# Feed-forwards with context by seven block products: two stages of a fused fp32 network on TensorE

## The chip, the cores and the metric

The kernel runs on one core of a Trainium2 chip. The metric is the device time of one execution in microseconds (us); lower is better. It is one launch, all weights come from HBM, and each fp32 operand of TensorE is split in a high part (of type fp32r) and a low part (the rest).

## What is computed

Two residual blocks in a row on 512 image tokens with 256 context tokens, model width 1024, hidden width 2816 (22 feature tiles of 128). A block has token mixers and gated feed-forwards, with modulation vectors made from a condition. Four feed-forwards are in the program. Two of them are applied to image and context tokens together (768 tokens): the first of block one, and that of the first layer of block two. These are the two that are changed.

```python
def rms_norm(x):
    xf = x.astype(jnp.float32)
    return (xf * lax.rsqrt(jnp.mean(xf * xf, axis=-1, keepdims=True) + RMS_EPS)).astype(x.dtype)

def modulate(x, shift, scale):
    return x * (1.0 + scale) + shift

def swiglu(x, wg, wu, wd):
    return (jax.nn.silu(x @ wg) * (x @ wu)) @ wd

def half_ffn(h, shift, scale, gate, wg, wu, wd):
    return h + 0.5 * gate * swiglu(modulate(rms_norm(h), shift, scale), wg, wu, wd)
```

## The kernel before

The stages run in the order filters, block1_ffn1, block1_mix, block1_ffn2, block2_mix0, block2_ffn0, block2_mix1, block2_ffn1, final. Each engine has a program of its own, and semaphores order them; the order of the work is written by hand. A matrix product is done as three products: high weights with high data, high weights with low data, low weights with high data.

Weights come as tiles of 128 x 1024 fp32 (512 KB) through one stream in HBM, in the order in which they are used. SyncE loads a tile in one of two raw buffers, ScalarE copies its high part in a ring of four (split_tile, L513), VectorE subtracts to get the low part (dve_low_tile, L527), and only then the raw buffer is free for the next load. In some stages GpSimd makes the low parts instead (L2780). Beside it SyncE loads the tiles of the modulation weights in two further buffers; VectorE multiplies each with the condition and sums it up, once for each of one or two vectors (dve_mod_tile, L570).

A feed-forward with context (pe_ffn, L826; act_ffn, L843; dve_ffn, L882) works in thirds of 8, 8 and 6 feature tiles. For each feature there is a gate tile and an up tile. A tile has 8 steps over the model width, three products in each, and two matmuls of 384 columns in each product, since 768 tokens lie in two banks of PSUM: 48 matmuls a tile. ScalarE takes silu of the gate (L852), VectorE multiplies it with the up part out of PSUM (L900), ScalarE and VectorE split the result in the hidden buffers (L859, L907). After a third come the 8 down tiles, each over the features of the third, and VectorE adds each output to the stream H (dve_residual, L952). PSUM has two slots of two banks for this, used in turn. Two modulation tiles go with each feature, and one with each output, in those loops for which the plan has them.

The stage begins with the norm: TensorE sums squares over the partitions, ScalarE makes the reciprocal root (L648, L651), VectorE scales a tile (L793, L798), ScalarE adds the shift and writes the high part (L732, L738), VectorE the low part (L776, L780). TensorE takes the first gate and up tile together, step by step, as the eight tiles of the input come (pe_pair, L435, matmuls at L457); all other tiles go through pe_tile (L410, matmuls at L427). The first four weight tiles are loaded and split during the filters stage (L1538, low parts on GpSimd at L2771), between the two layers of a small network whose sines ScalarE computes (L1544).

## Time and profile before

| | |
|---|---|
| time, median of 3 runs | 3512.42 us (3509.75 to 3512.66) |
| span of the profiled execution | 3513.3 us |
| TensorE busy | 3314.9 us (94%), 18356 matmuls |
| VectorE busy | 1987.9 us (57%) |
| ScalarE busy | 1152.1 us (33%) |
| GpSimd busy | 131.8 us (4%), 64 instructions |
| loads | 392 weight tiles and 168 modulation tiles of 512 KB |

The profile is of one execution. Its page names engines PE (TensorE's matmuls), PEld (its weight loads, which overlap the matmuls), DVE (VectorE), ACT (ScalarE), POOL (GpSimd) and SP (SyncE; SPq is its queue of DMA issues). Matmuls are pipelined and their ends are modelled, so that the duration of one in a row is longer than the pace at which they follow each other; the pace is the length of a stretch over the number in it. Stages are found by time: the first feed-forward with context runs from 160.5 to 712.8 us, the second from 2191 to 2743.7 us.

### The profile page before, as it was taken

The page shows a single profiled execution, that of the slowest core. Times are in us where ns is not written, and L with a number is a line of the kernel's source. Part 1 is how long each engine was busy: PE and PEld are TensorE (multiplying, and loading weights), DVE is VectorE, ACT ScalarE, POOL GpSimd, SP SyncE. Part 2 cuts the span into 40 slices and gives each one's busy share as a digit, 9 for nine tenths or more (in the row PEclk, how much of TensorE's full clock was granted, in tenths as well). Part 3 has the DMA queues.
Part 4 walks back from the last instruction along what each step waited for, and adds up shares of the span by engine and source line. Part 5 has one row for each costly group of instructions (what it writes and reads, how often), then busy time and mean ns, then how long its engine had stood idle before and what let it go on. Part 6 is the DMA issues. An engine that isn't in the chain of part 4 may idle for free.

```text
span 3513.3 us, 49004 instructions
## 1 busy us (share of the span) xinstructions
PE 3314.9 (94%) x18356; PEld 2879.2 (82%) x18356; DVE 1987.9 (57%) x2943; ACT 1152.1 (33%) x1604; POOL 131.8 (4%) x64
## 2 busy tenths in 40 slices
PE   6899999999999999999899889999999999789998
PEld 3599999988888887888688657999999767578887
DVE  6556443457766658884569573653433467653334
ACT  2221211235541133223435272311212344543223
POOL 3000000000000000000011100000000111000000
PEclk8799999999999999999989899999999989999999
DMA  5233332331122235553221202333322211113232
GB/s 217 100 120 133 125 130 78 115 108 38 36 82 81 82 127 178 191 192 108 68 72 31 77 3 72 105 134 120 132 96 66 81 43 43 43 60 98 93 96 96
DMA packets 101989, 339.95 MB, mean 97 GB/s; under 512 B 10351, under 2 KB 21487, under 8 KB 100432
## 3 DMA queue, kind: packets, MB, share of 16 engines
q1 hardware_dynamic: 82888, 301.91, 25.9%
q10 hardware_dynamic: 18952, 36.01, 2.9%
q8 instruction: 99, 1.62, 0.2%
q14 instruction: 50, 0.41, 0.0%
HBM read 323.73 MB, written 14.16 MB: 96 GB/s over the span
## 4 chain that ended last, share of the span: by engine, by line
PE 79%; DVE 10%; ACT 5%; issue 3%; DMA 2%; ACTq 1%; POOL 0%; SPq 0%; DVEq 0%; POOLq 0%
PE ps L427 62%; PE ps L473 5%; PE ps L457 2%; PE ps L1094 1%; ACT pr L2563 1%; DMA hyena_k<-fst 1%; PE ps L1956 1%; PE ps L1943 1%; PE ps L1042 1%; DVE u_ex L1240 1%; DVE u_Z L1354 1%; ACT pT L2570 1%; ACT wr_hi L524 1%; PE ps L1515 1%; DMA raw<-in_stream 1%
## 5 line engine op out<-in xcount | busy, mean ns | idle before, releaser
L524 ACT ACTIVATE wr_hi<-raw 128x1024 fp32r<-128x1024 f32 x388 | 411.8, 1061 | 601.1 <-PE ps L427 547.2
L534 DVE TENSOR_TENSOR wr_lo<-raw,wr_hi 128x1024 fp32r<-128x1024 f32 x348 | 426.2, 1225 | 80.6 <-ACT wr_hi L524 48.9
L900 DVE TENSOR_TENSOR ff_raw<-ps,ff_gate 128x768 f32<-128x768 f32 (+1 forms) x88 | 72.6, 825 | 571.0 <-PE ps L427 568.1
L427 PE MATMUL ps<-xx_hi,wr_hi 128*128 128x512 f32 x992 | 393.1, 396 | 2.0 <-ACT ff_gate L852 1.9
L427 PE MATMUL ps<-xx_lo,wr_hi 128*128 128x512 f32 x992 | 388.8, 392 | 0.0
L427 PE MATMUL ps<-xx_hi,wr_lo 128*128 128x512 f32 x992 | 388.5, 392 | 0.0
L427 PE MATMUL ps<-xa_hi,wr_hi 128*128 128x384 f32 x1344 | 341.0, 334 | 0.1
L427 PE MATMUL ps<-xa_lo,wr_hi 128*128 128x384 f32 x1344 | 341.0, 334 | 0.0
L427 PE MATMUL ps<-xa_hi,wr_lo 128*128 128x384 f32 x1344 | 341.0, 334 | 0.0
L578 DVE CUSTOM_DVE_ANT_0 ps<-raw,cb 128x1024 f32<-128x1024 f32 x240 | 295.4, 1231 | 54.1 <-DMA raw<-in_mod_stream 39.3
L427 PE MATMUL ps<-hid_hi,wr_hi 128*128 128x384 f32 (+1 forms) x1056 | 316.2, 353 | 3.8 <-DVE H L961 2.0
L427 PE MATMUL ps<-hid_lo,wr_hi 128*128 128x384 f32 (+1 forms) x1056 | 315.6, 352 | 0.0
L427 PE MATMUL ps<-hid_hi,wr_lo 128*128 128x384 f32 (+1 forms) x1056 | 315.5, 352 | 0.0
L427 PEld LDWEIGHTS ps<-xa_hi,wr_hi 128*128 128x128 f32 x1344 | 242.4, 188 | 0.6 <-issue 0.6
L427 PEld LDWEIGHTS ps<-xa_hi,wr_lo 128*128 128x128 f32 x1344 | 242.6, 188 | 0.0
L427 PEld LDWEIGHTS ps<-xa_lo,wr_hi 128*128 128x128 f32 x1344 | 242.6, 188 | 0.0
L859 ACT ACTIVATE hid_hi<-ff_raw 128x768 f32 (+1 forms) x88 | 65.2, 741 | 507.4 <-DVE ff_raw L900 507.3
L427 PEld LDWEIGHTS ps<-xx_hi,wr_hi 128*128 128x128 f32 x992 | 187.5, 189 | 44.3 <-issue 5.1
L427 PEld LDWEIGHTS ps<-xx_hi,wr_lo 128*128 128x128 f32 x992 | 187.3, 189 | 40.1
L427 PEld LDWEIGHTS ps<-xx_lo,wr_hi 128*128 128x128 f32 x992 | 187.5, 189 | 39.8 <-issue 0.8
L427 PEld LDWEIGHTS ps<-hid_hi,wr_hi 128*128 128x128 f32 x1056 | 193.0, 188 | 19.9 <-DVE hid_lo L907 2.7
L427 PEld LDWEIGHTS ps<-hid_hi,wr_lo 128*128 128x128 f32 x1056 | 193.2, 188 | 13.7
(417 smaller groups left out, 5327.3 us busy)
## 6 DMA issues: line engine op xcount, KB each, us to landing
raw<-in_stream SPq DMA_DIRECT2D x392, 512.0 KB, 3.6
raw<-in_mod_stream SPq DMA_DIRECT2D x168, 512.0 KB, 4.5
...
```

The costliest lines, as they stand in the source:

```text
L427: last = pe.matmul(gslot(slot)[:, col:col + n], w, rhs[part], start=(bi == 0 and pi == 0), stop=(bi == len(blocks) - 1 and pi == 2))
L457: last = pe.matmul(gslot(slots[t])[:, col:col + n], w, rhs[part], start=(k == 0 and pi == 0), stop=(k == steps - 1 and pi == 2))
L473: last = pe.matmul(gslot(slot)[:, col:col + n], w, rhs[part], start=(k == 0 and pi == 0), stop=(k == KC - 1 and pi == 2))
L524: act.activation(wr_hi[:, s, :], raw[:, s % RAW, :], ACT.Copy).then_inc(tile_hi, 1)
L534: dve.tensor_tensor(wr_lo[:, s, :], raw[:, s % RAW, :], wr_hi[:, s, :], ALU.subtract).then_inc(tile_lo, 1)
L578: ins = dve.tensor_tensor_reduce(out=product, in0=raw[:, RAW + place, :], in1=cb[:, v, :], scale=1.0, scalar=0.0, op0=ALU.mult, op1=ALU.ad ...
L859: act.activation(hid[0][:, bass.ds(i * 2 + q, 1), 0:n], ff_raw[:, q:q + 1, 0:n], ACT.Copy).then_inc(hhi_ready, 1)
L900: dve.tensor_tensor(parts(ff_raw[:, q, :], with_ctx), gparts(slot, with_ctx), parts(ff_gate[:, q, :], with_ctx), ALU.mult).then_inc(slot_f ...
L1042: last = pe.matmul(m[:, j * NX + c * HD:j * NX + (c + 1) * HD], Z[r, c * CH:(c + 1) * CH], queries[r, c * per:(c + 1) * per, 0 if bw else ...
L1094: last = pe.matmul(m[:, j * NX + c * HD:j * NX + (c + 1) * HD], Z[r, c * CH:(c + 1) * CH], queries[r, c * per:(c + 1) * per, 0 if bw else ...
L1240: dve.tensor_tensor(x, cum, a, ALU.subtract).then_inc(ex_in, 1)
L1354: dve.tensor_tensor(z[:, :, h, :], x[:, :, h, :], side[:, :, h, :], ALU.mult).then_inc(z_ready, 1)
```

## The change

In the two feed-forwards with context the products for a gate and an up tile are no longer done tile by tile. The pair of weight tiles is seen as a 2 x 2 matrix of blocks (gate or up; first or second half of the model width), the input as 2 x 2 blocks (half of the model width; half of the tokens), and the product of the two is made with seven block products and sums of blocks in place of eight. In detail:

- The input is prepared once in seven versions (units) of 4 x 384: some are blocks of it, four are made by 16 subtractions of 384 on GpSimd (pool_pair_norm). ScalarE and VectorE split all 28 parts in high and low. xn holds the scaled and shifted input, xs the seven versions.
- The weights of a pair are prepared in every round: the pair is loaded in both raw buffers, GpSimd makes four block sums of 512 (pool_pair_sums), ScalarE and VectorE split seven units of 512 in place of two tiles of 1024 (act_weights, dve_weights). Each unit of the next pair is written in its place of the ring once the product of this round that used it is done.
- A round on TensorE (pe_pair_round) is seven products of 4 steps x 3 matmuls of 384 columns. ScalarE copies the first three results out of PSUM, further products are added by TensorE in the same banks, and VectorE adds three banks to the copies (prod_summed); then silu, the two multiplications and the split of the hidden tile in two halves.
- Features go in groups of 4, 2, 4, 4, 4, 4 in place of 8, 8, 6, each group followed by its down products: four stream tiles, each for two outputs, over the features of the group. The sums into H come 48 times a stage in place of 24.
- Two modulation tiles stay with each feature, with two vectors or one; after the very first round they come behind the round's work, in all others ahead of it. Further ones lie in the down parts of some groups.
- Weights of gate and up come from an array of their own (pairs), the rest from the stream; TensorE's loops of these stages are written out. The first pair is prepared in the filters stage, with its low parts on GpSimd, and the pair for the second of these stages at the end of block2_mix0.

The diff, cut to its core:

```diff
+        def act_weights(act, tally, r, i):
+
+            sums = {1: 1, 2: 3, 4: 2, 5: 4}
+            if i in sums:
+                act.wait_ge(sum_ready, 4 * r + sums[i])
+            elif i == 0 or i == 6:
+                act.wait_ge(landed[i // 6], pair_landed(r, tally.n.get("tile_hi", 0)))
+            act.activation(unit_at(wr_hi, i), unit_raw(i), ACT.Copy).then_inc(unit_hi, 1)
+            act.wait_ge(unit_hi, PAIR_UNITS * r + i + 1)
+
+        def dve_weights(dve, r, i):
+            dve.wait_ge(unit_hi, PAIR_UNITS * r + i + 1)
+            dve.tensor_tensor(unit_at(wr_lo, i), unit_raw(i), unit_at(wr_hi, i), ALU.subtract).then_inc(unit_lo, 1)
+
+        def pool_pair_sums(pool, r, tiles):
+
+            gate_a, gate_b, up_a, up_b = raw[:, 0, 0:512], raw[:, 0, 512:1024], raw[:, 1, 0:512], raw[:, 1, 512:1024]
+            if r:
+                pool.wait_ge(unit_lo, PAIR_UNITS * (r - 1) + 2)
+            for s in range(RAW):
+                pool.wait_ge(landed[s], pair_landed(r, tiles))
+            nc.gpsimd.tensor_tensor(s_sum[:, :], up_a, up_b, ALU.add).then_inc(sum_ready, 1)
+            pool.wait_ge(sum_ready, 4 * r + 1)
+            nc.gpsimd.tensor_tensor(up_a, gate_a, up_a, ALU.subtract).then_inc(sum_ready, 1)
+            pool.wait_ge(sum_ready, 4 * r + 2)
...
+            pool.wait_ge(unit_lo, PAIR_UNITS * r + 1)
+            nc.gpsimd.tensor_tensor(gate_a, s_sum[:, :], gate_a, ALU.subtract).then_inc(sum_ready, 1)
...
+            pool.wait_ge(unit_lo, PAIR_UNITS * r + 4)
+            nc.gpsimd.tensor_tensor(gate_b, gate_b, gate_a, ALU.subtract).then_inc(sum_ready, 1)
...
+        def dve_pair_norm(dve, tally, which, shift, scale, gain=None, before=None):
...
+            for m in range(KC):
+                scaled(m)
+                if m:
+                    low((m - 1) // 4, (m - 1) % 4)
+            low(1, 3)
+            for u in range(2, PAIR_UNITS):
+                for j in range(4):
+                    low(u, j)
...
+        def pe_pair_round(pe, tally, r, which, first, begin):
+
+            for i in range(PAIR_UNITS):
+                pe.wait_ge(unit_lo, PAIR_UNITS * r + i + 1)
...
+                elif i == 1 and r:
+                    pe.wait_ge(prod_summed, 3 * r)
+                elif i == 2:
+                    pe.wait_ge(prod_copied, 3 * r + 1)
+                elif i == 3 and r:
+                    pe.wait_ge(prod_summed, 3 * (r - 1) + 1)
+                elif i == 4:
+                    pe.wait_ge(prod_copied, 3 * r + 3)
+                elif i == 5:
+                    pe.wait_ge(prod_copied, 3 * r + 2)
+                elif i == 6:
+                    pe.wait_ge(prod_summed, 3 * r + 2)
+                w_hi, w_lo = unit_at(wr_hi, i), unit_at(wr_lo, i)
+                for j in range(4):
+                    if first:
+                        pe.wait_ge(xs_ready, 4 * PAIR_UNITS * which + 4 * i + j + 1)
+                    for pi, (w, part) in enumerate(((w_hi, 0), (w_hi, 1), (w_lo, 0))):
+                        last = pe.matmul(pair_bank(r, i), w[:, j * P:(j + 1) * P], xs[part][:, i, j, :],
+                                         start=(i in (0, 1, 3) and j == 0 and pi == 0), stop=(j == 3 and pi == 2),
+                                         skip_group_check=True)
+                last.then_inc(prod_done, 1)
...
+            if not copied:
+                for n in range(3):
+                    act_prod_copy(act, tally, r, n)
+            high(0)
+            high(1)
+            act_gate(0)
+            high(2)
+            high(3)
+            if not then_down:
+                high(4)
+            act_gate(1)
+            if then_down:
+                high(4)
+            high(5)
+            act_hid(1)
+            act_hid(0)
+            high(6)
...
+        def dve_pair_round(dve, tally, r, f, then_down, later):
...
+            summed(0, gate0)
+            low(0)
+            low(1)
+            summed(1, up1)
+            low(2)
+            low(3)
+            summed(2, gate1)
+            low(4)
+            dve.wait_ge(prod_summed, 3 * r + 2)
+            dve.wait_ge(silu_ready, 2 * r + 2)
+            dve.tensor_tensor(gate1, up1, gate1, ALU.mult).then_inc(gated_half, 1)
+            low(5)
+            low_half(1, half_lo)
+            dve.wait_ge(prod_done, PAIR_UNITS * (r + 1))
+            dve.tensor_tensor(gate0, pair_bank(r, 6), gate0, ALU.mult).then_inc(gated_half, 1)
+            low_half(0, hid_ready)
+            tally.passed("hid_ready")
+            low(6)
+            if later is not None:
+                later()
...
+            def load_pair(r):
+                for s in range(RAW):
+                    sp.wait_ge(unit_lo, PAIR_UNITS * r + s - 1)
+                    sp.dma_start(raw[:, s, :], ins["pairs"][2 * r + s]).then_inc(landed[s], 16)
...
+PAIR_GROUPS = (4, 2, 4, 4, 4, 4)
+PAIR_UNITS = 7
+PAIR_MODS = (((2, 0), (2, 0), (2, 2), (1, 1), (1, 1), (1, 0)), ((2, 2), (2, 0), (1, 0), (1, 0), (1, 0), (1, 0)))
```

## Rows read from the trace of the kernel before

**Rows 1.** The page, busy us (share of the span) xinstructions of each engine.

```profile
PE 3314.9 (94%) x18356; PEld 2879.2 (82%) x18356; DVE 1987.9 (57%) x2943; ACT 1152.1 (33%) x1604; POOL 131.8 (4%) x64
```

**Rows 2.** The chain that ended last: start us, us, what.

```profile
160.58 19.47 PE ps L457 x96
180.04 532.72 PE ps L427 x3072
...
2210.88 532.73 PE ps L427 x3072
```

**Rows 3.** Windows, the first feed-forward with context: length, busy us of each engine, clock.

```profile
160.50:712.80 552.30, 552.22 (x3169) 551.78 (x3170) 275.23 (x368) 128.68 (x137) 0.00 (x0) 0.99 0.34 115
```

**Rows 4.** Timeline, start of the second such stage: start us, us, engine, line.

```profile
2188.93 0.75 DVE L793 SCALAR_TENSOR_TENSOR xt<-H,scv,rstd 128x512 f32<-128x512 f32 x1 [2.92 <-ACT rstd L651]
...
2191.18 0.98 PE L457 MATMUL ps<-xa_hi,wr_hi 128*128 128x384 f32 x2 [4.23 <-ACT xa_hi L738]
...
2197.10 0.51 PE L457 MATMUL ps<-xa_hi,wr_hi 128*128 128x384 f32 x2
```

**Rows 5.** Groups by line and form, first stage: xcount, busy us, mean ns, idle before.

```profile
L578 DVE CUSTOM_DVE_ANT_0 ps<-raw,cb 128x1024 f32<-128x1024 f32 x80 | 98.4, 1230 | 20.1 <-DMA raw<-in_mod_stream 16.6 <-DVE mods L590 2.4 <-DVE xa_lo L780 0.3
```

**Rows 6.** Durations of 512 and 384 wide work: two groups by form, two timeline rows.

```profile
L2135 DVE TENSOR_TENSOR y_lo<-hyp,y_hi 128x512 fp32r<-128x512 f32 x8 | 5.5, 684 | 0.0
...
L859 ACT ACTIVATE hid_hi<-ff_raw 128x512 f32 x44 | 27.9, 634 | 190.7 <-DVE ff_raw L900 190.6
...
1798.20 0.56 DVE L1354 TENSOR_TENSOR u_Z<-u_ex,gk 128x384 f32<-128x384 f32 x1
1798.68 0.55 DVE L1354 TENSOR_TENSOR u_Z<-u_ex,gq 128x384 f32<-128x384 f32 x1
```

**Rows 7.** Timeline of VectorE, a modulation tile with two vectors and what follows.

```profile
249.09 1.23 DVE L578 CUSTOM_DVE_ANT_0 ps<-raw,cb 128x1024 f32<-128x1024 f32 x1
...
250.41 1.23 DVE L578 CUSTOM_DVE_ANT_0 ps<-raw,cb 128x1024 f32<-128x1024 f32 x1
...
251.94 0.96 DVE L907 TENSOR_TENSOR hid_lo<-ff_raw,hid_hi 128x768 f32 x1 [0.25 <-DVE modacc L578]
```

**Rows 8.** Groups by form, GpSimd.

```profile
L2780 POOL TENSOR_TENSOR wr_lo<-raw,wr_hi 128x1024 fp32r<-128x1024 f32 x40 | 96.5, 2414 | 2821.7 <-ACT wr_hi L524 2821.7
L1600 POOL TENSOR_TENSOR ssq_first<-ssq_first,sq_first 128x768 f32<-128x768 f32 x7 | 13.7, 1961 | 25.3 <-ACT sq_first L1583 25.3
```

**Rows 9.** Timelines of GpSimd and VectorE, three places where both work.

```profile
47.40 6.28 POOL L1597 TENSOR_TENSOR H<-H,pos_col 128x512 f32<-128x512 f32 x4
48.02 1.64 DVE L1642 TENSOR_TENSOR fe<-fa 128x512 f32<-128x512 f32 x1
...
60.53 1.94 POOL L1600 TENSOR_TENSOR ssq_first<-ssq_first,sq_first 128x768 f32<-128x768 f32 x1 [6.85 <-ACT sq_first L1583]
60.84 2.71 DVE L578 CUSTOM_DVE_ANT_0 mod_out<-raw,cb 128x1024 f32<-128x1024 f32 x1
...
1791.93 2.42 POOL L2780 TENSOR_TENSOR wr_lo<-raw,wr_hi 128x1024 fp32r<-128x1024 f32 x1 [6.14 <-ACT wr_hi L524]
1792.56 0.96 DVE L2344 SCALAR_TENSOR_TENSOR oacc<-ps,oacc 128x768 f32<-128x768 f32 x1 [0.41 <-PE ps L2167]
```

**Rows 10.** A load on SyncE's queue, and the issues: KB each, median us to landing.

```profile
2185.88 0.33 SPq L2747 DMA_DIRECT2D raw<-in_stream  x1
...
raw<-in_stream SPq DMA_DIRECT2D x392, 512.0 KB, 3.6
```

**Rows 11.** Timeline of the filters stage, VectorE and ScalarE around the second layer's sine.

```profile
22.48 0.43 DVE L1625 TENSOR_SCALAR fh<-fh 128x512 f32<-128x512 f32 x1
...
24.52 1.06 ACT L1538 ACTIVATE wr_hi<-raw 128x1024 fp32r<-128x1024 f32 x1 [7.48 <-DMA raw<-in_stream]
...
26.90 1.91 ACT L563 ACTIVATE cb<-cb 128x2048 f32<-128x2048 f32 x1
...
28.84 0.63 ACT L1544 ACTIVATE fh<-fh 128x512 f32<-128x512 f32 x1
```

481 lines of the change are left out of this document (398 added, 83 removed).

## Prediction, written before the changed kernel was run

> **What bounds the kernel now.** I read the page's busy table first: TensorE is busy 94% of the span, VectorE 57%, GpSimd 4% [rows 1]. The chain of work that ended last says where that is a bound: in each of the two feed-forwards with context the chain is one unbroken piece of 3072 matmuls in 532.7 us, after a piece of 96 in 19.5 us that starts it [rows 2]. So there TensorE issues one 384-column matmul every 532.72/3072 = 173.4 ns and waits for nobody. The window of the first stage shows the rest: in 552.3 us VectorE works 275 us, ScalarE 129 us, GpSimd not at all [rows 3]. VectorE is half idle, but it is the only other engine with much work, and in the first feed-forward the modulation products alone (80 of 1.23 us) are a third of it [rows 5]. What is to be asked of the change is not whether TensorE gets less work (it does), but whether VectorE, GpSimd and the loads still keep up with it.
>
> **Removed.** A pair of gate and up tiles takes 2 x 8 x 2 x 3 = 96 matmuls; seven products of 4 steps x 3 take 84. Down products stay 24 features x columns as before (22 x 8 x 2 x 3 = 1056). Over 22 pairs and two stages 528 matmuls go: 528 x 0.1734 = 91.6 us. The pace should hold, since it does not depend on the loop around it (the same 173.4 ns in both stages). A round of 84 now lasts 14.57 us, and all of the following has to fit beside that.
>
> **VectorE in a round.** Durations: 512-wide subtraction 0.69 us, 384-wide 0.55, and such instructions follow each other 0.08 us closer than their durations [rows 6]. Seven weight units 7 x 0.61 = 4.3; three sums from PSUM, two multiplications, two low halves, 7 x 0.47 = 3.3; two modulation tiles of two vectors 2 x 2.85 = 5.7 (with one vector 3.1, a product less for each tile, 1.32), read from start to next start [rows 7]; a wait of about 0.65 for ScalarE's high half in the last half tile. Sum 14.0 us (11.4 with one vector) of 14.57. Alone it would fit, just.
>
> **GpSimd in a round.** Four 512-wide operations. Its 1024-wide took 2.41 us and 768-wide 1.96 [rows 8], so 1.15 to 1.25 each, 4.8 us a round. First what the trace shows of the two engines together: with GpSimd running from 60.53 to 62.47, a modulation product of VectorE that starts at 60.84 takes 2.71 us in place of 1.23, so it lost 1.48 of the 1.63 us of overlap; a subtraction in SBUF took 1.64 us beside a stream of GpSimd work, in place of 0.69; an operation with one operand in PSUM took 0.96 beside GpSimd, its usual time [rows 9]. So lows, low halves, one multiplication and modulations (11.5 us a round) take turns with GpSimd, the sums from PSUM don't. About 1 us of the 4.8 falls beside those; I add 3.5. The Trainium skill (SBUF — State Buffer, "SBUF: two separate sides") says the shared port pair is an exclusive lock for a whole instruction against VectorE operations with two SBUF inputs; by it all 4.8 would be added, 1.2 us more for each of the some ten rounds bound by VectorE, 12 us in all: 3551. The row has the loss slightly under that, and the sum goes by the row.
>
> **The loop through the load.** The pair for the round after next is loaded once the last unit of this one is split. From there: issue and landing (0.33 and 3.6 [rows 10], 4.1 with the way to both queues), two sums on GpSimd, the third (which waits for VectorE's unit 0), ScalarE's unit 2 (0.63), VectorE's units 2 and 3, the fourth sum, ScalarE's and VectorE's unit 5, then the low half, the last multiplication, ScalarE's half tile, the low half, unit 6. Counted on one clock from "unit 6 split": loads landed 4.1; sums 5.3 and 6.5 to 7.5; third sum 8.6 (9.9 with two vectors); unit 2 at 9.9 (11.1); unit 3 10.5 (11.7); fourth sum 11.7 (12.9); unit 5 13.3 (14.5); unit 6 16.1 (17.2). So a round is 16.1 us with one vector and 17.2 with two, against TensorE's 14.57.
>
> **What of that reaches TensorE.** Product 6 waits for the second PSUM sum (8.0 or 9.2 on that clock; allowed 12.5 us into TensorE's round), and product 2 waits for ScalarE's copy of product 0, which is queued behind the previous round's unit 6 (16.6, or 17.7; allowed 4.2 into the next round). After a group of down products VectorE starts 2.1 us behind. A group of four with one vector: behind 4.1, 5.7, 5.7 us at its next rounds; stalls 0, 0, 1.5, 1.5: 3 us. With two vectors: 4.7, 5.9, 5.9; stalls 1.45, 2.65, 1.75, and 2.5 at the down products' last feature (hidden features come ready 22 us after the round began, the first three features cover 3.1): 8.3, taken as 9 since the group before it leaves VectorE later. The group of two has only one feature (1.04 us) as cover: 5.1, and 1.4 more because its outputs come every 2.08 us against 1.9 of VectorE's work: 6.5. First stage: 6.5 + 9 + 3 x 3 = 24.5. Second: 6.5 + 4 x 3 = 18.5.
>
> **The start of a stage.** Before, the first matmul comes 2.25 us after VectorE's first instruction, and 96 take 19.4 us, 2.7 over their pace, a part of them at the 1.2 GHz level (0.98 us for two, later 0.51) [rows 4]. After, VectorE makes 8 scaled tiles and 28 low parts, ScalarE 16 biased and 28 high parts, GpSimd 16 sums of 384 (0.93 each). For the first eight steps VectorE needs 1.18 + 0.47 and gives way to one GpSimd operation (0.85 less gaps): 2.25 us each, to 19.7 us. Then 20 low parts and 10 to 11 GpSimd operations in turn: to 38.9. Only behind them in its queue stand the first sums: product 6 starts at 41.2 and ends at 43.2. Without the turn-taking it would be 35. The 84 matmuls need 2.25 + 14.57 = 16.8; loss 26.4, less the 2.7 of before: 23.7. Then VectorE has two rounds of modulations in a row (11.4 plus two GpSimd sums): the next product 6 waits to 65.2 where it could start at 55.7: 9.5. The third round 2.65, the last 1.75 + 2.5. A stage's first group: 40.1 us, two of them 80.2. Bounds: 26 without turn-taking, 46 if VectorE loses every turn.
>
> **The filters.** The second pair of raw tiles falls away there: ScalarE waited 7.5 us for it, and the second layer's sine at 28.84 was queued behind it and the 1.9 us silu, while its argument was ready at 22.9 [rows 11]. Gain 6, less 2 for three more weight copies and GpSimd's chain in front of the absolute values: 4 us (bounds 7 and -2). Down instructions: 24 more residuals per stage, 1.2 us each, lie beside 4.16 us of matmuls per output: nothing, as long as VectorE is not already behind.
>
> **Sum.** 3513.3 - 91.6 + 80.2 + 24.5 + 18.5 - 4 = 3540.9 for the profiled execution, which lies 0.9 over the median: 3540.
>
> **Rivals.**
> A, faster: turn-taking costs little, since GpSimd's sums fall into VectorE's waits for TensorE. Then only the start costs, 26 to 27 us per stage, and 1 at each group of two: 3513 - 92 + 55 - 4 = 3472; with half of the turn-taking 3500. For it: VectorE's own sum, 14.0 of 14.57. Against it: rows 9, and the 16 us loop for the load, which is there with few turns too (15.1).
> B, slower still: TensorE's clock. It ran at its 2.4 GHz level throughout the two stages and at 1.2 for 5.6 us after each gap in front of them [rows 3, 4]. With gaps of 2 to 9 us in some twelve rounds, 5.6 us at half rate cost 2.8 each; most lie inside rounds that wait for VectorE anyway. It decides from gaps in front of down products (five of them) and at the start: 15 to 35 more, 3565.
> C, none to see: the bounds of the start (26) with the groups as worked out: 3513 - 92 + 52 + 43 - 4 = 3512.
> D, the seven products don't keep the pace of 173.4 ns, each having its own start and one bank: 2% on 3700 matmuls would be 13 us. Nothing in the rows speaks for it.
>
> **Numbers.** Forecast 0.44 (3515 to 3560), A 0.34 (3468 to 3505), B with D 0.14, C 0.08. A change of 0.2%, 7 us, is about what a measurement can tell. Slower 0.56 (nearly all of the forecast, B and D), same 0.09 (most of C), faster 0.35 (A and a rest of C). The range takes in A and B: 3465 to 3578. The forecast's own range is 3515 to 3560.
>
> **What would show it.** In the profile after: 528 matmuls fewer at the same 173 ns; TensorE waiting for VectorE's sums (product 6) and ScalarE's copies (product 2), in the first group of each stage for over 25 us; GpSimd at about 370 us busy in place of 132 (176 pair sums of 1.2 and 32 of 0.93 on top); VectorE's 512-wide subtractions at a mean well over 0.69 us in these stages (0.9 or more), its PSUM sums at 0.55. Wrong if the subtractions keep 0.69, if rounds come every 14.6 us in groups two to six, or if the first round ends under 36 us after VectorE's first instruction; then it is A.

## The result, and the profile after

The changed kernel takes 3595.69 us (median of four, 3589.35 to 3601.39), the kernel before on the same chip 3511.09 (3508.38 to 3512.66): ratio 1.0248, 95% interval 1.0225 to 1.0270. It is slower by some 85 us. The profiled execution has a span of 3589.2 us, 75.9 over that of before.

Page of the changed kernel: span, busy us (share) xinstructions of each engine, to be held against [rows 1].

```profile
span 3589.2 us, 48360 instructions
...
PE 3277.0 (91%) x17828; PEld 2814.0 (78%) x17828; DVE 2307.1 (64%) x3500; ACT 1362.6 (38%) x2097; POOL 430.1 (12%) x275
```

The 528 matmuls are gone. Window of the first feed-forward with context (length, then busy us of PE, PEld, DVE, ACT, POOL, granted clock), to be held against [rows 3]:

```profile
154.60:760.50 605.90, 545.84 (x2912) 527.50 (x2912) 438.56 (x653) 235.59 (x384) 145.49 (x100) 0.94 0.33 108
```

VectorE went from 275 to 439 us in that stage, GpSimd from 0 to 145, the granted clock from 0.99 to 0.94, and TensorE, which waited for nobody, now waits. TensorE's longest waits (us in total, times, longest):

```profile
PE ps L1135 <- ACT gh L1168: 45.4, 31, 2.5
PE ps L1135 <- DVE xs_lo L1070: 29.5, 24, 7.4
PE ps L440 <- DVE hs_lo L1307: 28.9, 12, 4.8
...
PE ps L1135 <- DVE gh L1313: 13.8, 7, 5.7
```

L1135 is the products' line, L440 the down products'. The first wait is product 2 for ScalarE's copy of product 0, the second the start of a stage, the third the first output of each of twelve down groups, the last one shown product 6 for the PSUM sums.

From the starts of TensorE's rounds I take one number per piece of a stage, its *lateness*: time until the next piece starts, less its matmuls at 173.4 ns. A one-vector group is one whose modulation tiles are multiplied for one vector. Four rows of such a group, the starts of its second, third and fourth round and of its down products:

```profile
571.14 0.33 PE L1135 MATMUL ps<-xs_hi,wr_hi 128*128 128x384 f32 x1
...
586.79 0.34 PE L1135 MATMUL ps<-xs_hi,wr_hi 128*128 128x384 f32 x1
...
605.13 0.33 PE L1135 MATMUL ps<-xs_hi,wr_hi 128*128 128x384 f32 x1
...
620.79 0.33 PE L440 MATMUL ps<-hs_hi,wr_hi 128*128 128x384 f32 x1
```

The rounds took 15.65, 18.34 and 15.66 us against 14.57: late by 1.1, 3.8 and 1.1. Summed over both stages, with what the prediction's steps give in the same pieces:

| us, both stages | first round | second round | other 40 rounds | down products | sum |
|---|---|---|---|---|---|
| predicted | 52.8 | 19.0 | 36.3 | 20.5 | 128.6 |
| measured | 49.0 | 23.6 | 65.2 | 45.2 | 183.0 |

Of the 183.0, some 33 are matmuls that follow each other at 0.32 us in place of 0.173, TensorE's lower clock level: 11.7 in the first two columns, 12.4 in the other rounds, 8.8 in the down products. The account closes: 91.6 removed, 183.0 added, 5.3 of before's own lateness gone, 10.3 less outside the two stages: +75.8 against 75.9 measured.

### The profile page after: what moved, and what is told of

It reads as the page before. It is cut to its first block, busy times and chain, and to the rows that moved or that the text cites. A ratio compares the mean times of both kernels' runs of the same rounds, so it can differ in the third digit from the quotient of the medians.

```text
span 3589.2 us, 48360 instructions
## 1 busy us (share of the span) xinstructions
PE 3277.0 (91%) x17828; PEld 2814.0 (78%) x17828; DVE 2307.1 (64%) x3500; ACT 1362.6 (38%) x2097; POOL 430.1 (12%) x275
## 4 chain that ended last, share of the span: by engine, by line
PE 62%; DVE 18%; ACT 8%; issue 7%; DMA 3%; POOL 2%; ACTq 1%; SPq 0%; DVEq 0%; POOLq 0%
PE ps L440 40%; PE ps L1135 6%; PE ps L486 5%; DVE wr_lo L979 2%; ACT hs_hi L1185 1%; PE ps L1483 1%; ACT wr_hi L974 1%; DVE xs_lo L1070 1%; POOL raw L995 1%; ACT pr L2952 1%; DMA hyena_k<-fst 1%; DMA raw<-in_pairs 1%; PE ps L2345 1%; PE ps L2332 1%; PE ps L470 1%
## 5 line engine op out<-in xcount | busy, mean ns | idle before, releaser
L1135 PE MATMUL ps<-xs_hi,wr_hi 128*128 128x384 f32 x1232 | 436.4, 354 | 93.6 <-ACT gh L1168 45.4
L1135 PE MATMUL ps<-xs_hi,wr_lo 128*128 128x384 f32 x1232 | 427.4, 347 | 0.0
L1135 PE MATMUL ps<-xs_lo,wr_hi 128*128 128x384 f32 x1232 | 427.4, 347 | 0.0
L440 PE MATMUL ps<-xx_hi,wr_hi 128*128 128x512 f32 x992 | 393.4, 397 | 1.7 <-ACT ff_gate L857 1.7
L440 PE MATMUL ps<-xx_lo,wr_hi 128*128 128x512 f32 x992 | 389.5, 393 | 0.0
L440 PE MATMUL ps<-xx_hi,wr_lo 128*128 128x512 f32 x992 | 389.0, 392 | 0.0
L1135 PEld LDWEIGHTS ps<-xs_hi,wr_hi 128*128 128x128 f32 x1232 | 242.0, 196 | 122.4 <-issue 75.9
L587 DVE CUSTOM_DVE_ANT_0 ps<-raw,cb 128x1024 f32<-128x1024 f32 x240 | 305.3, 1272 | 19.2 <-DMA raw<-in_mod_stream 8.0
L543 DVE TENSOR_TENSOR wr_lo<-raw,wr_hi 128x1024 fp32r<-128x1024 f32 x216 | 264.4, 1225 | 64.5 <-ACT wr_hi L533 48.7
L979 DVE TENSOR_TENSOR wr_lo<-raw,wr_hi 128x512 fp32r<-128x512 f32 x258 | 213.0, 836 | 47.4 <-ACT wr_hi L974 42.6
L1135 PEld LDWEIGHTS ps<-xs_lo,wr_hi 128*128 128x128 f32 x1232 | 243.1, 197 | 0.0
L1135 PEld LDWEIGHTS ps<-xs_hi,wr_lo 128*128 128x128 f32 x1232 | 242.8, 197 | 0.0
L440 PEld LDWEIGHTS ps<-xx_hi,wr_hi 128*128 128x128 f32 x992 | 187.3, 189 | 43.9 <-issue 4.8
L440 PEld LDWEIGHTS ps<-xx_hi,wr_lo 128*128 128x128 f32 x992 | 187.3, 189 | 40.2
L440 PEld LDWEIGHTS ps<-xx_lo,wr_hi 128*128 128x128 f32 x992 | 187.5, 189 | 39.8 <-issue 0.8
L440 PE MATMUL ps<-hs_hi,wr_hi 128*128 128x384 f32 x704 | 184.2, 343 | 31.3 <-DVE hs_lo L1307 28.9
L440 PE MATMUL ps<-hs_lo,wr_hi 128*128 128x384 f32 x704 | 182.6, 341 | 0.0
L440 PE MATMUL ps<-hs_hi,wr_lo 128*128 128x384 f32 x704 | 182.4, 340 | 0.0
```

The costliest lines, as they stand in the source:

```text
L440: last = pe.matmul(gslot(slot)[:, col:col + n], w, rhs[part], start=(bi == 0 and pi == 0), stop=(bi == len(blocks) - 1 and pi == 2))
L543: dve.tensor_tensor(wr_lo[:, s, :], raw[:, s % RAW, :], wr_hi[:, s, :], ALU.subtract).then_inc(tile_lo, 1)
L587: ins = dve.tensor_tensor_reduce(out=product, in0=raw[:, RAW + place, :], in1=cb[:, v, :], scale=1.0, scalar=0.0, op0=ALU.mult, op1=ALU.ad ...
L979: dve.tensor_tensor(unit_at(wr_lo, i), unit_raw(i), unit_at(wr_hi, i), ALU.subtract).then_inc(unit_lo, 1)
L1135: last = pe.matmul(pair_bank(r, i), w[:, j * P:(j + 1) * P], xs[part][:, i, j, :], start=(i in (0, 1, 3) and j == 0 and pi == 0), stop=(j ...
```

## The experiments

Four theories. **S**: the rounds are set by a loop of hand-overs in which GpSimd's four sums stand. **V**: VectorE has too much work, or loses it to turns with GpSimd. **L**: what counts in the loop is the pair's load. **C**: what hurts is TensorE's clock. For the second round and the stage's start, **Q** is the order of queues. All kernels, with time, ratio to before on the same chip, and lateness by piece from one profile each:

| kernel | us | ratio [95%] | first | second | others | down | sum |
|---|---|---|---|---|---|---|---|
| changed | 3595.7 | 1.0248 [1.0225, 1.0270] | 49.0 | 23.6 | 65.2 | 45.2 | 183.0 |
| e1_pair_sums_8_wide | 3523.4 | 1.0047 [1.0026, 1.0069] | 45.7 | 16.2 | 0.7 | 47.0 | 109.5 |
| e2_input_sums_8_wide | 3591.4 | 1.0241 [1.0220, 1.0262] | 37.5 | 19.6 | 65.1 | 48.6 | 170.8 |
| e3_round_mods_8_wide | 3585.5 | 1.0219 [1.0197, 1.0241] | 49.1 | 15.1 | 63.4 | 45.2 | 172.8 |
| e4_sums_on_vector | 3557.9 | 1.0142 [1.0121, 1.0163] | 52.6 | 18.3 | 27.3 | 45.3 | 143.5 |
| e5_copy_before_unit6 | 3606.7 | 1.0269 [1.0242, 1.0296] | 50.3 | 22.9 | 62.1 | 51.9 | 187.2 |
| e6_pair_memsets | 3604.4 | 1.0271 [1.0251, 1.0291] | 45.7 | 22.4 | 72.0 | 52.9 | 193.0 |
| e7_small_pair_load | 3589.6 | 1.0229 [1.0206, 1.0252] | 49.1 | 22.6 | 51.5 | 50.3 | 173.4 |
| e9_vector_sums_order | 3574.1 | 1.0181 [1.0155, 1.0208] | 52.6 | 21.0 | 31.3 | 55.2 | 160.1 |
| e10_two_memsets | 3538.0 | 1.0091 [1.0069, 1.0113] | 45.8 | 19.2 | 13.2 | 46.0 | 124.1 |
| e11_xs_low_8_wide | 3591.6 | 1.0233 [1.0211, 1.0254] | 42.3 | 20.6 | 67.9 | 47.0 | 177.8 |
| e12_first_mods_8_wide | 3593.7 | 1.0240 [1.0220, 1.0260] | 49.7 | 17.2 | 67.0 | 47.8 | 181.6 |
| e13_down_cover | 3547.4 | 1.0118 [1.0098, 1.0138] | 51.7 | 19.2 | 26.4 | 35.8 | 133.2 |
| e14_pair_load_first | 3597.4 | 1.0244 [1.0227, 1.0261] | 49.1 | 21.8 | 63.0 | 46.9 | 180.7 |
| e15_first_mods_and_load | 3591.6 | 1.0229 [1.0212, 1.0246] | 49.1 | 7.8 | 68.2 | 45.2 | 170.4 |
| e16_best | 3560.5 | 1.0132 [1.0116, 1.0149] | 52.1 | 19.3 | 36.1 | 37.2 | 144.7 |
| e17_two_sums_each | 3573.3 | 1.0178 [1.0160, 1.0197] | 52.2 | 21.3 | 36.2 | 53.6 | 163.2 |
| e18_vector_sums_small_load | 3544.8 | 1.0098 [1.0076, 1.0121] | 52.6 | 18.4 | 16.6 | 48.7 | 136.3 |
| e19_cover_and_load_first | 3551.4 | 1.0113 [1.0091, 1.0134] | 52.6 | 18.3 | 26.0 | 35.6 | 132.6 |

The intervals of e2, e3, e5, e6, e7, e11, e12, e14 and e15 overlap that of the changed kernel, so that by time alone none of these is shown to differ from it; what is said of them rests on the pieces of one profile each. e1, e2, e3, e6, e7, e10, e11, e12, e15 and e18 leave a part of the work out.

### GpSimd's pair sums: gone, replaced by settings without reads, shorter

```diff
 # e1: all pairs but the first of a stage
+w = 8 if r % sum(PAIR_GROUPS) else 512
-nc.gpsimd.tensor_tensor(s_sum[:, :], up_a, up_b, ALU.add)
+nc.gpsimd.tensor_tensor(s_sum[:, 0:w], up_a, up_b, ALU.add)
 # e6: each sum becomes three settings (e10: two), one behind the other
-nc.gpsimd.tensor_tensor(s_sum[:, :], up_a, up_b, ALU.add)
+for _ in range(3):
+    nc.gpsimd.memset(s_sum[:, :], 0.5)
```

> GpSimd's four block sums of a pair work on 8 columns in place of 512 (but for the first pair of each stage), so that they cost neither time nor VectorE's turn; all waits stay, and part of the weights is not summed. Theory S (the sums hold the rounds, by their own 1.3 to 1.6 us in the chain and by the turns they take from VectorE): of some 50 us that a stage loses to waits of TensorE behind its first group, about 35 go, and some 3 of the second round's 11.6: time 3515 to 3530 in place of 3596, subtractions of 512 back at 0.69 us. Theory V (VectorE's own load of sums, lows and modulations holds them): rounds with two vectors stay at 17 to 18 us and the time at 3570 or more. Theory C (TensorE's clock after each wait): it falls away only with the waits, no time of its own.

> The changed kernel; each of GpSimd's four sums of a pair (all pairs but the first) is replaced by three settings of the same 512 columns to a constant, one behind the other: GpSimd stays busy about as long, in the same places and with the same waits, but reads nothing from SBUF, so the weights of those pairs are meaningless. It parts the length of the sums from their turn-taking with VectorE. If the length of GpSimd's steps in the chain is what costs: VectorE's subtractions go back to about 0.7 us, and yet the rounds stay over 1 us late each, 3570 to 3590 us. If turn-taking (long sums because VectorE holds them up, long subtractions because GpSimd does) is what costs: the rounds fall to within 0.5 us of 14.6 and the time to 3525 to 3545 us.

> As the kernel with three settings in place of each of GpSimd's pair sums, but with two: about 1.1 us for each sum in place of 1.6, no reads of SBUF, so the weights of those pairs are meaningless. 1.1 us is a sum at its own length, without turn-taking. Theory T (what costs is how long GpSimd's step in the chain is, and turn-taking costs by making that step 1.5 us in place of 1.15): the one-vector rounds, late by 1.2, 4.3 and 1.3 us with three settings, come down to about 0.6, 1.5, 1.0, as with the sums on VectorE; 3560 to 3575 us. If the number of hand-overs between the queues is what costs, and not the length: no change from three settings, 3595 to 3605 us.

With the sums all but gone (e1) the other rounds come at their pace (0.7 us in 40) and 72 of the 85 us are back. Which property of the sums it is, e6 and e10 were to say. Groups by form in e6's first stage (count, busy, mean ns, idle before):

```profile
L994 POOL MEMSET raw<- 128x512 f32 x126 | 66.4, 527 | 79.5 <-DVE wr_lo L980 73.9
...
L980 DVE TENSOR_TENSOR wr_lo<-raw,wr_hi 128x512 fp32r<-128x512 f32 x126 | 85.6, 689 | 42.8 <-ACT wr_hi L975 40.5
```

and the same subtractions in the changed kernel:

```profile
L979 DVE TENSOR_TENSOR wr_lo<-raw,wr_hi 128x512 fp32r<-128x512 f32 x126 | 104.9, 843 | 23.9 <-ACT wr_hi L974 21.5
```

Without GpSimd reads VectorE lost nothing (689 ns, as in [rows 6]) and got some 19 us a stage back in these subtractions, and the kernel was no faster. A GpSimd step of e6 is longer than the sum that it stands for: 1.70 us from the start of its first setting to the end of its third, against 1.41 to 1.61 on average. In e10 it is 1.11 us (two settings), the other rounds fell from 72.0 to 13.2 and the time from 3604 to 3538 us. One loop of e10, GpSimd's steps and SyncE's issues:

```profile
555.86 0.53 POOL L994 MEMSET s_sum<- 128x512 f32 x1 [8.28 <-DMA raw<-in_pairs]
556.44 0.53 POOL L997 MEMSET s_sum<- 128x512 f32 x1
...
561.56 0.53 POOL L994 MEMSET raw<- 128x512 f32 x1 [2.26 <-DVE wr_lo L980]
562.14 0.53 POOL L997 MEMSET raw<- 128x512 f32 x1
```

```profile
549.08 3.27 SPq L3140 DMA_DIRECT2D raw<-in_pairs  x2
...
564.17 3.27 SPq L3140 DMA_DIRECT2D raw<-in_pairs  x2
```

So the length of GpSimd's steps decides, and what VectorE loses weighs little: that V holds the one-vector rounds falls, and e3 agrees, where narrow modulation products leave most of these rounds at 1.1, 3.7 and 1.1. How much of a step's length is turn-taking e10 does not say. Its 1.11 us is not "a sum at its own length", as its expectation has it: the changed kernel's 512-wide sums take 1.26 to 1.31 us where VectorE does not hold them up. So e10 takes away more than the turns, and a kernel whose sums keep 1.26 to 1.31 us was not built. My e10 expectation (3560 to 3575) gave the length too little weight: 0.6 us more in each of four steps costs 66 us, since it exceeds what room the loop has, repeats every round and brings the clock down with it (43.0 us lost at the lower level in e6, 19.1 in e10).

> The modulation products that stand in the rounds of the two stages work on 8 columns in place of 1024 (their loads and waits stay; the modulation vectors come out wrong). Theory S: rounds with one vector don't change (15.6 and 18.3 us in turn), those with two lose at most 1 to 2 us, and the second round of a stage, in front of which two rounds' modulations stand, loses 8 to 10 of its 11.6 us wait: 3596 less 2 x 9 less some 8 = 3565 to 3575. Theory V: all rounds go to 14.6 to 15 us: 3515 to 3530.

```diff
 # e3: width of the products of the modulation tiles in rounds; most of each product left out
-dve_mod_tile(dve, tally, 2 * (f % 2) + n, vectors, mslot(0))
+dve_mod_tile(dve, tally, 2 * (f % 2) + n, vectors, mslot(0), 8)
```

S had expected too much of it; it took 8.5 us of lateness out of the second round and little elsewhere.

### The loop, step by step

Timeline of the changed kernel over one of its loops (start us, us, engine, line), from one load of a pair to the next. Each fence is one engine: SyncE's issues, GpSimd, ScalarE, VectorE.

```profile
573.29 3.41 SPq L3129 DMA_DIRECT2D raw<-in_pairs  x2
...
590.09 3.40 SPq L3129 DMA_DIRECT2D raw<-in_pairs  x2
```

```profile
580.17 1.29 POOL L988 TENSOR_TENSOR s_sum<-raw 128x512 f32<-128x512 f32 x1 [8.53 <-DMA raw<-in_pairs]
581.55 1.62 POOL L990 TENSOR_TENSOR raw<-raw 128x512 f32<-128x512 f32 x1
583.25 1.62 POOL L995 TENSOR_TENSOR raw<-s_sum,raw 128x512 f32<-128x512 f32 x1
587.15 1.29 POOL L1001 TENSOR_TENSOR raw<-raw 128x512 f32<-128x512 f32 x1 [2.28 <-DVE wr_lo L979]
```

```profile
584.98 1.96 ACT L974 ACTIVATE wr_hi<-raw 128x512 fp32r<-128x512 f32 x3 [2.21 <-PE ps L1135]
...
591.79 0.63 ACT L974 ACTIVATE wr_hi<-raw 128x512 fp32r<-128x512 f32 x1
592.45 1.01 ACT L1168 ACTIVATE gh<-ps 128x384 f32<-128x384 f32 x2
```

```profile
585.65 1.36 DVE L979 TENSOR_TENSOR wr_lo<-raw,wr_hi 128x512 fp32r<-128x512 f32 x2 [1.46 <-ACT wr_hi L974]
...
587.39 1.60 DVE L979 TENSOR_TENSOR wr_lo<-raw,wr_hi 128x512 fp32r<-128x512 f32 x1
...
592.45 0.69 DVE L979 TENSOR_TENSOR wr_lo<-raw,wr_hi 128x512 fp32r<-128x512 f32 x1
```

The second half of a pair is issued at 576.37 (576.70 less 0.33), when unit 6 is split. On that clock: landed 3.8, sums done 5.1 and 6.8, third sum 8.5, unit 3 split 10.6, fourth sum 12.1, unit 6 split 16.8; the next issue is at 593.16, 16.79 later. The prediction had 4.1, 5.3, up to 7.5, 8.6, 10.5, 11.7, 16.1. It is the same loop, 0.7 us longer. The four sums take 5.8 us in place of the 4.8 reckoned for them (four of 1.29 would be 5.2, so 0.6 to 0.7 is turn-taking), but up to the third sum the two clocks agree (8.5 and 8.6), since the forecast had the second end as late as 7.5; the 0.7 comes behind it, 0.2 to unit 3, 0.3 in the fourth sum and 0.3 from there to unit 6, where VectorE's subtraction of 1.60 us stands.

In e10 the issues lie 15.09 apart; the prediction had 15.1 without turns. Of the 1.7 us between the two kernels' loops 1.4 are GpSimd's steps (5.8 against 4.4) and 0.3 the stretch behind the fourth (4.7 against 4.4). And behind unit 6 in ScalarE's queue stand two copies; when the first is done, product 2 starts:

```profile
593.08 0.41 PE L1135 MATMUL ps<-xs_hi,wr_hi 128*128 128x384 f32 x1 [1.96 <-ACT gh L1168]
...
594.70 0.52 PE L1135 MATMUL ps<-xs_hi,wr_lo 128*128 128x384 f32 x1
595.02 0.52 PE L1135 MATMUL ps<-xs_hi,wr_hi 128*128 128x384 f32 x1
```

A good microsecond after that wait the matmuls follow each other at 0.32 us, ten times, and the window shows the granted clock there (columns as in the window above; 1.00 is the 2.4 GHz level, 0.52 all but wholly the 1.2 GHz one):

```profile
590.00:593.00 3.00, 1.12 (x7) 0.80 (x5) 2.20 (x5) 1.75 (x5) 0.00 (x0) 1.00 0.55 175
594.20:597.60 3.40, 3.40 (x13) 3.40 (x13) 1.63 (x4) 1.12 (x2) 0.72 (x1) 0.52 0.91 302
```

This is the 3.8 us round: 2.2 of waiting and 1.5 of slow matmuls. Each group of four behind a stage's first has one or two such stretches, in a round or in its down products. No run changes the clock by itself, so C is measured only as its share of a profile, not tested: how much of the time would come back if the waits stayed and the clock did not fall is open.

### Other ways to shorten the loop

```diff
 # e4: pairs behind the first of a group; e17: only sums 3 and 4 move
-pool_pair_sums(pool, r, tiles)          # each round
+pair_sum(0); pair_sum(1)                # VectorE, ahead of the first PSUM sum
+pair_sum(2)                             # behind unit 0; pair_sum(3) behind unit 3
 # e7, e18: loads within a group
-sp.dma_start(raw[:, s, :], ins["pairs"][2 * r + s])
+sp.dma_start(raw[:, s, 0:64], ins["pairs"][2 * r + s][:, 0:64])
```

> The four pair sums move from GpSimd to VectorE, except for the first pair of each group: two ahead of the first PSUM sum, the third behind unit 0, the fourth behind unit 3. VectorE gets 4 x 0.61 = 2.4 us more in a round; GpSimd takes no turns in it. Theory S: the chain from product 3 to the next round's product 2 is shorter by about 2 us (0.61 for 1.3 to 1.6 twice, no subtraction held up by 0.9): one-vector rounds 15 us in place of 15.6 to 18.3, two-vector rounds 16 to 17 in place of 17 to 18: 3596 less 2 x 12 = 3570 to 3580. Theory V: VectorE was full, and the time rises by up to 2 us a round: 3610 to 3640.

> The changed kernel with only the third and fourth sum of a pair moved to VectorE (but for the first pair of each group). Everything is computed. Theory S (only GpSimd's steps inside the chain cost, about 1.5 us each against VectorE's 0.7): at least as good as all four on VectorE (3557.9 us), 3543 to 3556 us. Theory V (turn-taking with VectorE costs wherever GpSimd works, since VectorE has little room): 3565 to 3580 us.

> The changed kernel; the loads of a pair of gate and up tiles within a group bring 64 of 1024 columns of each tile (the rest of the buffer keeps old values, so these weights are meaningless). Theory S (GpSimd's sums and the queue behind them): the load lands ahead of its need except in the first sum of a round, which has room; 3585 to 3597 us. Theory L (the loop runs through the buffer's load, as the prediction reckoned it at 16.1 and 17.2 us): the load shortens by about 1 to 2 us, and so does each round over 14.6 us; 3550 to 3570 us.

> The kernel with the pair sums on VectorE (3557.9 us), its pair loads within a group bringing 64 of 1024 columns of each tile (these weights are meaningless); that takes the way from issue to landing from 3.6 to 1.7 us. In the trace of the kernel with the sums on VectorE, VectorE waits 0.9 and 1.8 us for that load ahead of the first sum. Theory L (once the sums are short, what is left of the rounds' lateness, 0.3 to 1.0 us with one vector and 1.9 and 2.6 with two, is the loop through the load): the one-vector rounds come within 0.2 us of 14.57, the two-vector ones within 1; 3535 to 3545 us. Theory V (VectorE's work itself is what is left): 3552 to 3560 us.

On VectorE a sum takes 0.69 us, and though it is given the work, the kernel gains 38 us (e4). I then took the first two sums to have room, and moved only the other two (e17): it lost 15 us against e4. Its timeline shows that they have none:

```profile
571.92 1.29 POOL L988 TENSOR_TENSOR s_sum<-raw 128x512 f32<-128x512 f32 x1 [14.16 <-DMA raw<-in_pairs]
...
573.29 1.62 POOL L990 TENSOR_TENSOR raw<-raw 128x512 f32<-128x512 f32 x1
...
574.94 0.69 DVE L1302 TENSOR_TENSOR raw<-s_sum,raw 128x512 f32<-128x512 f32 x1 [1.18 <-POOL raw L990]
```

The first starts when the load lands, and VectorE waits for the second. In e4 VectorE itself waits for the load:

```profile
586.67 0.69 DVE L1305 TENSOR_TENSOR s_sum<-raw 128x512 f32<-128x512 f32 x1 [1.78 <-DMA raw<-in_pairs]
```

So the load is in the loop. Alone, cut from 3.6 to 1.7 us of landing (e7), it gives 13.7 us in the other rounds, of which the down products lose 5.1 again; most one-vector rounds then stand at 15.6 to 15.8, all three of a group alike, since a second loop without the load binds:

```profile
576.75 1.61 POOL L995 TENSOR_TENSOR raw<-s_sum,raw 128x512 f32<-128x512 f32 x1 [0.77 <-DVE wr_lo L979]
```

There the third sum waits for unit 0, which in VectorE's queue stands behind the PSUM sum of product 3, which comes after product 2, which waited for the copy behind unit 6. Load and sums both short (e18) leave one-vector rounds mostly 0.3 us late, and two-vector rounds at 1.9 and 2.6 as in e4. There VectorE's own work is more than a round (14.0 us reckoned and 2.4 of sums, against 14.57), so that it is probably the bound; no run takes work from VectorE in e18 to show it.

```diff
 # e5, e9 (e9: with e4): ScalarE's order
 act_hid(0)
+act_prod_copy(act, tally, r + 1, 0)
 high(6)
```

> The changed kernel with one step of ScalarE's order moved: the copy of the next round's product 0, which TensorE's product 2 waits for, stands ahead of the split of unit 6 and not behind it. Everything is computed. Theory S (the in-order chain through GpSimd's sums, ending in ScalarE's queue: unit 6, then the copy): the copy starts about 0.6 us earlier in each of some 36 rounds that follow another, unit 6 comes 0.6 us later, which may then be what is late; 0.2 to 0.5 us a round come back, 3577 to 3590 us. If the order in ScalarE's queue is nothing (VectorE's work or the clock sets the pace): 3590 to 3600 us.

> The two orders together: the pair sums on VectorE (but for the first pair of each group, which stays on GpSimd) and ScalarE's copy of the next round's product 0 ahead of unit 6. Everything is computed. With the sums on VectorE alone the time was 3557.9 us and the rounds 0.3 to 2.6 us over 14.57. Theory S: the queue's end is the same, 0.1 to 0.4 us of each round come back, 3545 to 3555 us. Theory V (VectorE is the bound in these rounds: it has 14.0 us of work and the four sums more): nothing comes back, 3556 to 3560 us. In no case under the 3511 us of before, since the start of each stage keeps about 35 us.

Neither gained: e9 was 16 us slower than e4, e5 11 us slower than the changed kernel, with intervals that overlap. Product 0 of the next round is only done 2.1 us into it, so unit 6, now behind its copy, waits for TensorE: product 2's wait in a one-vector round falls from 1.0 to 0.3, product 6's grows by up to 0.9, and down products start later. The order was not the fault.

### The start of a stage, and the second round

```diff
 # e2: GpSimd's 16 input sums, here the first four
-nc.gpsimd.tensor_tensor(xn[:, j, 0, :], xn[:, j, 1, :], xn[:, j, 0, :], ALU.subtract)
+nc.gpsimd.tensor_tensor(xn[:, j, 0, 0:8], xn[:, j, 1, 0:8], xn[:, j, 0, 0:8], ALU.subtract)
 # e11: VectorE's low parts; TensorE reads xs[part if i < 2 else 0]
+w = 8 if u >= 2 else half_tokens
-dve.tensor_tensor(xs[1][:, u, j, :], xs_source(u, j), xs[0][:, u, j, :], ALU.subtract)
+dve.tensor_tensor(xs[1][:, u, j, 0:w], xs_source(u, j)[:, 0:w], xs[0][:, u, j, 0:w], ALU.subtract)
 # e12: columns of the modulation products in rounds
-dve_mod_tile(dve, tally, 2 * (f % 2) + n, vectors, mslot(0))
+dve_mod_tile(dve, tally, 2 * (f % 2) + n, vectors, mslot(0), D if g or f > 1 else 8)
 # e14: first group of a stage, SyncE (e15: e12 and e14 together)
+load_pair(r + 1)
 next_mods(2)
-load_pair(r + 1)
```

> The 16 block subtractions of the input on GpSimd work on 8 columns in place of 384, at the start of both stages; the pair sums stay. Theory S: the first low parts of the input, 38.5 us after VectorE's first instruction, are all there after 29 to 31, and TensorE's first round (39.1 us) lasts 30 to 32: 3596 less 2 x 8 = 3580. If ScalarE's chain (biased and high parts) sets the first eight steps, they stay at 2.27 us each and only the part behind them shrinks: 34 to 35 us, 3588. If the input sums don't matter: 3596.

> The changed kernel; at the start of each stage the 20 low parts of the inputs of products 2 to 6 are made on 8 of their 384 columns, and TensorE reads the high part in their place (the same number of matmuls of the same size; their result is meaningless). It takes some 16 us of work out of VectorE's queue, ahead of the first sums. Theory S (the first round is bound by VectorE's queue in turns with GpSimd's input sums): the first round, late by 24.5 us, comes down to about 15, the second stays near 11; 3573 to 3580 us. If the first round is bound by ScalarE's or GpSimd's own chain of sums, copies and high parts: 2 us at most a stage, 3588 to 3596 us.

> The changed kernel; the four modulation tiles that VectorE makes behind the first round and ahead of the second round's sums, in each stage, are multiplied on 8 of 1024 columns (modulation values wrong). It takes about 10 us out of VectorE's queue between the first and the second round. Theory S (the second round's 11.6 us are the modulations of two rounds in a row): it falls to 2 to 4 us, both stages together 3578 to 3584 us. If the second round is late because of GpSimd's sums of its next pair and the chain behind them: 3590 to 3596 us.

> The changed kernel with one step of SyncE's order moved, in the first group of each stage: the load of the third pair of gate and up tiles is issued ahead of the second round's modulation tiles, not behind them. Everything is computed. In the changed kernel its buffer is free at 204.1 us of the profile and it is issued at 209.7, behind two modulation loads that wait for VectorE. Theory Q (the second round is late by two chains of like length, VectorE's eight modulation products to 215.7 us and the late pair with GpSimd's sums behind it): alone it gives back what the sums lie behind, 1 to 3 us a stage, 3588 to 3594 us. If the load does not matter: 3593 to 3600 us.

> Both at once: the pair load issued first, and the four modulation tiles ahead of the second round's sums multiplied on 8 of 1024 columns (modulation values wrong). The narrow products alone left the second round 7.1 and 9.9 us late. Theory Q: with both chains shortened it falls to 2 to 4 us in each stage, 3578 to 3585 us. If something else holds the second round (ScalarE's table load and silu, GpSimd): it stays at 7 to 10 us, 3590 to 3594 us.

The first round ends 42.9 us after VectorE's first instruction (197.48 less 154.60). Taking GpSimd out (e2) gives 11.5 us in two stages, taking 16 us of VectorE's queue out (e11) only 6.7, less than half of what I expected: neither engine's part alone holds the start. In e2 the first eight steps come every 1.84 us, in e11 still every 2.28; and behind them, in e11, ScalarE works without a gap from 174.99 to 187.67, high parts and copies, before it reaches the next pair.

The second round was put down to VectorE's two rounds of modulation products. Those alone (e12) gave 6.4 us of its lateness in two stages, the load alone (e14) 1.8, both together (e15) 15.8. So two chains of like length end together. SyncE's issues in the changed kernel, and ScalarE behind them:

```profile
206.71 2.98 SPq L3124 DMA_DIRECT2D raw<-in_mod_stream  x2
209.73 0.91 SPq L3129 DMA_DIRECT2D raw<-in_pairs  x2
...
214.45 0.63 ACT L974 ACTIVATE wr_hi<-raw 128x512 fp32r<-128x512 f32 x1 [6.53 <-DMA raw<-in_pairs]
```

VectorE's last product ends at 215.76, and the pair, free to be loaded at 204.2, was issued at 209.73 behind two modulation loads that wait for VectorE. In e15 its first half goes out at 203.59. Of the 15.8 us, 3 are lost again in the other rounds. The medians of e15 and the changed kernel lie only 4 us apart, within the spread of the runs, and e14's is not lower at all, where I expected 3578 to 3585 and 3588 to 3594: the pieces of one profile each and not the time carry this finding.

### The down products, and the best that came of it

```diff
 # e13 (with e4), e16, e19: first down tile of a group
-for each output: features 0 .. F-1
+features 0 .. F-2 of output 0, then of output 1 (once its bank is free), then the last of both
```

> The kernel with the pair sums on VectorE (3557.9 us), and in the first down tile of each group TensorE works on two outputs in turn: all features but the last of both, then the last of both. Everything is computed. In every kernel so far, also in the one with 8-column sums whose rounds came each 14.56 us, the first output waits 2.0 to 2.3 us in a group of four and 5.4 to 6 in a group of two for the group's last hidden feature. Theory S: that is the fixed way from product 6 over VectorE and ScalarE to the last low half, about 5.2 us, with three features (3.1 us) as cover. The second output's bank comes free about 1.5 us before the feature is there, so 1.3 to 2 us come back in each of the twelve groups: 3534 to 3544 us. If VectorE, being behind, then makes the later outputs wait for their banks: 3552 to 3560 us.

> Three repairs together, everything computed: of a pair's four sums GpSimd keeps the first two, which have room, and VectorE makes the third and fourth, which stand in the chain from unit 0 to unit 2 and from unit 3 to unit 5; the first down tile takes its two outputs in turn; the pair load goes first in the first group. By theory S rounds come 0 to 0.4 us late (0.3 to 1.0 with all four sums on VectorE), so this is 5 to 15 us under the 3547.4 us of all sums on VectorE with the down tile in turn: 3532 to 3542 us. If GpSimd's two sums still hold up VectorE's modulation products enough to matter: 3545 to 3555 us. The starts of the stages stay (over 30 us each), so in no case under 3511 us.

> Pair sums on VectorE, first down tile with its two outputs in turn, and the third pair's load issued ahead of two modulation tiles in the first group. Everything is computed. The first two together took 3547.4 us. The load alone changed the second round from 11.6 to 10.8 us late and nothing else; here VectorE's sums wait in its queue for that load, so more may come back: 0 to 3 us, 3543 to 3548 us. Under the 3511 us of before in no case.

In every kernel with the old order, e1 included, TensorE's first output stands still for at least 1.9 us more than the pace in a group of four and 4.0 to 5.8 in a group of two (changed kernel, first output of a group of four, then VectorE's last low half):

```profile
626.12 0.61 PE L440 MATMUL ps<-hs_hi,wr_hi 128*128 128x384 f32 x2 [2.05 <-DVE hs_lo L1307]
```

```profile
624.31 0.55 DVE L1329 TENSOR_TENSOR gh<-ps,gh 128x384 f32<-128x384 f32 x1
625.51 0.56 DVE L1307 TENSOR_TENSOR hs_lo<-gh,hs_hi 128x384 fp32r<-128x384 f32 x1 [0.65 <-ACT hs_hi L1185]
```

The products end at 620.8, the last low half at 626.07: 5.3 us, against 3.1 us of features 0 to 2. It is a fixed way, there even where nobody is behind. e13 gives 9.5 us of it back in twelve groups, less than I had expected; TensorE then still waits 0.88 us (the third group of four, at 605.11) ahead of the last feature. e16 keeps two sums on GpSimd as e17 does and came slower than either range that I had given (3560.5 us; 3532 to 3542 or 3545 to 3555), and e19 adds nothing to e13. Despite e16's name, the best complete kernel is e13: at 3547.4 us it is 48 us faster than the changed kernel and 1.18% slower than before. Nothing built here beats the kernel before.

## Why the prediction was off

The forecast (3540, 3515 to 3560) had the side right and the size short by 56 us; the measured time lies outside the range. In the profile lateness is 54.4 us over the forecast's: 28.9 in the other rounds (12.4 of it the lower clock level, 16.5 waits), 24.7 in the down products (8.8 and 15.9), and 0.8 in the first and second rounds together. So three terms of the sum were too small: what the loop leaves for TensorE to wait, the cover at the down products, and the clock, which the forecast put at nothing beyond before's own start. The rest of the difference lies outside the stages (6 us less than forecast) and in the profiled execution, whose span is 6.5 us under the median where 0.9 over it was reckoned.

- **Removed, pace.** Right: 528 matmuls, and in e1 a round of 84 takes 14.56 us. Rival D is out.
- **The filters.** VectorE's first instruction of the first stage comes 3.7 us earlier (154.60; before 160.58 less 2.25); 4 were forecast. Of the 10.3 us less outside the stages, 2.2 lie there (3.7, less 1.5 by which the first matmul follows later on VectorE); 3.1 between the stages and 5.0 behind the second are not explained.
- **Start of a stage.** Right within 2 us a stage: low parts end 38.5 us after VectorE's first instruction (38.9 forecast), the round at 42.9 (43.2), and a first group costs 41 us over before's (40.1). The second round, 11.8 a stage for 9.5, lacked the pair's load, which I had not followed through SyncE's queue past the modulation loads.
- **The loop through the load.** The step that failed first, by its size: 16.1 us forecast, 16.8 measured. The chain and its places were right to some tenths. But the sums stood in it at 1.15 to 1.25 us, where a 512-wide one takes 1.26 at the least, and the turn-taking of [rows 9] was charged to VectorE only, as 3.5 us a round. Groups by form of the changed kernel, first stage:

```profile
L995 POOL TENSOR_TENSOR raw<-s_sum,raw 128x512 f32<-128x512 f32 x21 | 33.8, 1609 | 18.2 <-DVE wr_lo L979 17.7
L990 POOL TENSOR_TENSOR raw<-raw 128x512 f32<-128x512 f32 x21 | 31.4, 1496 | 1.6
L988 POOL TENSOR_TENSOR s_sum<-raw 128x512 f32<-128x512 f32 x21 | 30.0, 1429 | 309.2 <-DMA raw<-in_pairs 309.2
L1001 POOL TENSOR_TENSOR raw<-raw 128x512 f32<-128x512 f32 x21 | 29.7, 1412 | 66.3 <-DVE wr_lo L979 66.3
```

  A turn costs whoever comes second, and the one whose place in the loop it is was mostly GpSimd: 1.41 to 1.61 us. e10, with 1.1 us a step, comes out at 3538.0 us and 124.1 of lateness, near the forecast's 3540 and 128.6, but by chance: 13.2 in the other rounds against 36.3 forecast, and 46.0 in the down products against 20.5.
- **What of it reaches TensorE.** 36.3 forecast for the other rounds, 65.2 measured. Stalls in the four rounds of a one-vector group were to be 0, 0, 1.5 and 1.5; they are 0, 1.1, 3.8 and 1.1, the third with 1.5 of the lower clock level. The second round was to have room. That it has none is the loop without the load, which the forecast did not have: e7 leaves each of these rounds at about 1.1 with the load almost gone.
- **Down products.** 20.5 forecast, 45.2 measured. In one-vector groups I let the last feature come in time; it takes 5.3 us from the last product and has 3.1 us of cover, so 2.0 to 2.3 us in each of those groups (seven), without the clock. The group of two was right but for the clock: 8.0 us, 6.3 and 6.8 without the slow matmuls, for 6.5. 8.8 us of the 45.2 are the clock.
- **Rival B**, the clock, was right as a mechanism: some 33 us measured where it had 15 to 35, of which 11.7 lie in the first two rounds, where it is not shown what they add to the waits. It came together with the rest and not in its stead, and after gaps of about 2 us. **A** is refuted: VectorE's subtractions grew to 843 ns and the rounds are late. It had one thing right, that what VectorE itself loses weighs little (e6); the price was GpSimd's. **C** needed a first group of 26 us; it was 41.
- **The signs named in advance**: waits for copies, sums and the start as said; GpSimd at 430 us (370 forecast; 176 sums at 1.2 took some 50 us more, 32 at 0.93 some 12); PSUM sums at 553 ns as said; SBUF subtractions at 843 (0.9 or more forecast).
- **The rule on the port.** A subtraction starting at 587.39 beside a GpSimd sum of 587.15 to 588.44 ends 0.55 us after it, so that it lost 0.91 us of 1.05 beside it; beside memory settings it kept 689 ns. The Trainium skill (SBUF — State Buffer, "SBUF: two separate sides") says that the lock holds for a whole instruction, that whichever of the two engines starts first has it while the other waits, and that, for a VectorE operation with two SBUF inputs, it holds only against a GpSimd operation that reads SBUF. With that rule the traces agree: GpSimd's sums grew too, from 1.29 to 1.62 us. My 3551 from it fell short like 3540, since both took only VectorE's half of the rule.
